# Two views of the rows, 64 bytes apart, and weights that begin 64 bytes later

## The reference

```
y = modulate(rmsnorm(h), sh, sc);  h = h + 0.5 * gt * swiglu(y, w_gu, w_down)     # D_FF = 2816
proj = modulate(rmsnorm(h), ...) @ w_in        # q, k, v, gu, gv: attention and gated mixing
h = h + gt2 * (merged @ w_out);                # then a second swiglu, then rmsnorm
```

## Time and profile before

| | us |
|---|---|
| median of 3 runs | 2518.12 (2514.95 to 2522.17) |
| the profiled execution, its own time | 2518.71 |
| its span, from first to last instruction | 2516.9 |
| TensorE matmuls busy | 2442.9 (97%) |
| VectorE busy | 1515.5 (60%) |
| ScalarE busy | 893.3 (35%) |
| GpSimd busy | 380.7 (15%) |

### The profile page before, as it was taken

The page is one execution under the profiler, slowest core; times in us unless marked ns, Lnnn a source line. Parts: engine busy times, 40 slices in busy tenths (PEclk is TensorE's granted clock), DMA queues, the critical chain, the costliest instruction groups (busy, mean ns, idle before and its releaser), DMA issues.

```text
span 2516.9 us, 39335 instructions
## 1 busy us (share of the span) xinstructions
PE 2442.9 (97%) x14736; PEld 2165.5 (86%) x14736; DVE 1515.5 (60%) x2434; ACT 893.3 (35%) x1103; POOL 380.7 (15%) x353
## 2 busy tenths in 40 slices
PE   6999989999999998999999999999999999999999
PEld 5998879999888888867778888888888889999999
DVE  7676767967877765355477776642222364555444
ACT  4443554444222223332232222232222242254443
POOL 2110531211111102332211111001110001000110
PEclk7999989999999999999999999999999999999999
DMA  7877745854655554211135545422222342234545
GB/s 279 277 260 268 260 140 199 272 196 167 209 192 200 175 167 153 80 63 51 67 119 198 197 170 191 161 101 89 94 84 97 104 143 84 68 118 151 184 168 166
DMA packets 79878, 400.19 MB, mean 159 GB/s; under 512 B 8816, under 2 KB 12912, under 8 KB 54704
## 3 DMA queue, kind: packets, MB, share of 16 engines
q1 hardware_dynamic: 77216, 393.39, 45.3%
q0 software_dynamic: 1056, 3.67, 0.4%
q10 hardware_dynamic: 1520, 1.95, 0.2%
HBM read 396.88 MB, written 2.10 MB: 159 GB/s over the span
## 4 chain that ended last, share of the span: by engine, by line
PE 85%; DVE 7%; ACT 3%; DMA 3%; issue 2%; POOL 0%; ACTq 0%; SPq 0%; DVEq 0%; POOLq 0%
PE pg L1159 24%; PE pg L1161 24%; PE pg L1160 24%; DMA raw<-w_d 2%; PE pg L1335 2%; PE pg L1336 2%; PE pg L1337 2%; DVE wlo L2049 1%; PE px L1977 1%; DMA raw<-w_t 1%; ACT whi L662 1%; DVE ada L2089 1%; PE px L1738 1%; PE pg L1777 1%; PE px L1963 1%
## 5 line engine op out<-in xcount | busy, mean ns | idle before, releaser
L1159 PE MATMUL pg<-Yh,whi 128*128 128x256 f32 (+1 forms) x2856 | 958.6, 336 | 27.5 <-DVE Yl L2209 7.6
L1160 PE MATMUL pg<-Yl,whi 128*128 128x256 f32 (+1 forms) x2856 | 948.5, 332 | 0.0
L1161 PE MATMUL pg<-Yh,wlo 128*128 128x256 f32 (+1 forms) x2856 | 948.3, 332 | 0.0
L2054 DVE TENSOR_TENSOR wlo<-raw,whi 128x2048 fp32r<-128x2048 f32 (+1 forms) x202 | 415.0, 2055 | 517.7 <-ACT whi L667 517.0
L1159 PEld LDWEIGHTS pg<-Yh,whi 128*128 128x128 f32 x2856 | 548.0, 192 | 90.4 <-issue 20.9
L1161 PEld LDWEIGHTS pg<-Yh,wlo 128*128 128x128 f32 x2856 | 548.1, 192 | 50.1
L1160 PEld LDWEIGHTS pg<-Yl,whi 128*128 128x128 f32 x2856 | 548.4, 192 | 49.0
L667 ACT ACTIVATE whi<-raw 128x2048 fp32r<-128x2048 f32 (+1 forms) x202 | 348.4, 1725 | 563.8 <-PE pg L1161 521.8
L1159 PE MATMUL pg<-Hh,whi 128*128 128x256 f32 (+1 forms) x1122 | 368.9, 329 | 4.7 <-DVE wlo L2054 3.2
L1160 PE MATMUL pg<-Hl,whi 128*128 128x256 f32 (+1 forms) x1122 | 366.4, 327 | 0.0
L1161 PE MATMUL pg<-Hh,wlo 128*128 128x256 f32 (+1 forms) x1122 | 366.4, 327 | 0.0
(11 more groups left out here) (352 smaller groups left out, 2354.8 us busy)
## 6 DMA issues: line engine op xcount, KB each, us to landing
raw<-w_t SPq DMA_DIRECT2D x194, 1024.0 KB, 5.0
ada<-w_ada SPq DMA_DIRECT2D x200, 512.0 KB, 3.6
raw<-w_d SPq DMA_DIRECT2D x96, 704.0 KB, 4.1
ADA<-w_ada SPq DMA_DIRECT2D x16, 512.0 KB, 14.6
NB<-na_bias POOLq DMA_DIRECT2D x8, 256.0 KB, 2.9
X<-x_t ACTq DMA_DIRECT2D x2, 512.0 KB, 16.7
spectrum<-HF POOLq DMA_DIRECT2D x1, 1024.0 KB, 9.2
X<-ctx_t SPq DMA_DIRECT2D x1, 1024.0 KB, 7.4
```

The source lines that it names most:

```text
L1159: pe.matmul(out, w_hi, y_hi, start=first, stop=False)
L1160: pe.matmul(out, w_hi, y_lo, start=False, stop=False)
L1161: return pe.matmul(out, w_lo, y_hi, start=False, stop=last)
L2054: dve.tensor_tensor(wlo[:, n % 2, 0:size], raw[:, n % 2, 0:size], whi[:, n % 2, 0:size].bitcast(F32), ALU.subtract)\
```

## The change

No instruction is added, removed or moved. The tensors' places change:

- A second view of the rows, YhB and YlB, begins 64 bytes after Yh and Yl, and a second view of the hidden rows, HhB and HlB, 64 bytes after Hh and Hl. Each pair shares its memory; 128 bytes of room follow each tensor.
- `row_view(name)` gives the B views for the norms and phases in SHORT_ROWS, that is where the phase has 256 columns, and for l1_in, whose products have 512 columns only for k; otherwise the views as before. `inner_of(name)` does the same for the hidden rows by the phase's column count. All writes and reads of the rows go through them.
- raw, whi and wlo begin 64 bytes past a multiple of 128, and another 64 bytes follow wlo, so that ada and all behind it keep their place modulo 128.
- The tensors of layer 1's mixer (K3, VN3 and those behind, with OH and OL laid over them) begin 64 bytes later in the region.
- HF, DF0 and HP, which use idle halves of the rows' memory early on, move with the B views.

```diff
@@ -183,6 +183,8 @@
 
     return 18 * list(LEAD).index(name) + {"added": 1, "inverse": 2, "scaled": 2 * c + 2 if c else 3, "lo": min(2 * c + 5, 18)}[step]
 
+SHORT_ROWS = ("b1_0", "b1_gu1", "b1_1", "b1_in", "merge", "b1_out", "b1_2", "b1_gu2", "l1_1", "l1_in", "l1_2", "l1_gu2")
+
 READS = {"b1_gu1": "b1_0", "b1_in": "b1_1", "b1_out": "merge", "b1_gu2": "b1_2", "l0_gu1": "l0_0", "l0_in": "l0_1",
          "l0_gu2": "l0_2", "l1_gu1": "l1_0", "l1_in": "l1_1", "l1_gu2": "l1_2"}
 
@@ -204,10 +206,17 @@
     X = sb("X", [P, KD, 512])
     y_at = at[0]
     Yh = sb("Yh", [P, 4096], F32R)
+    YhB = nc.alloc_sbuf_tensor_at("YhB", [P, 4096], F32R, offset=y_at + 64)
+    at[0] += 128
+    yl_at = at[0]
     Yl = sb("Yl", [P, 4096], F32R)
+    YlB = nc.alloc_sbuf_tensor_at("YlB", [P, 4096], F32R, offset=yl_at + 64)
+    at[0] += 128
+    at[0] += 64
     raw = sb("raw", [P, 2, BLK])
     whi = sb("whi", [P, 2, BLK], F32R)
     wlo = sb("wlo", [P, 2, BLK], F32R)
+    at[0] += 64
     ada = sb("ada", [P, 2, KD * P])
     V = sb("V", [P, NVEC])
     MOD = sb("MOD", [P, 216, 2])
@@ -225,15 +234,21 @@
     def over(): at[0] = region
 
     Hh = sb("Hh", [P, KF, 512], F32R)
+    HhB = nc.alloc_sbuf_tensor_at("HhB", [P, KF, 512], F32R, offset=region + 64)
+    at[0] += 128
+    hl_at = at[0]
     Hl = sb("Hl", [P, KF, 512], F32R)
+    HlB = nc.alloc_sbuf_tensor_at("HlB", [P, KF, 512], F32R, offset=hl_at + 64)
+    at[0] += 64
+    assert at[0] <= end
 
     over()
     EMB = sb("EMB", [64, 256]); FW1 = sb("FW1", [64, 64]); FW23 = sb("FW23", [64, 2, 64]); FW4 = sb("FW4", [64, 1024])
     FA = sb("FA", [64, 256]); FK = sb("FK", [64, 256]); FS = sb("FS", [64, 3, 256])
     WIN = sb("WIN", [P, 2, 512]); HN = sb("HN", [P, 2, 1024]); CS = sb("CS", [P, 1024])
-    HF = nc.alloc_sbuf_tensor_at("HF", [P, 8, 512], F32, offset=y_at)[:, :, 256:512]
-    DF0 = nc.alloc_sbuf_tensor_at("DF0", [P, 8, 512], F32, offset=y_at + 16384)[:, 2:6, 256:512]
-    taps = nc.alloc_sbuf_tensor_at("HP", [P, 22, 512], F32, offset=region)
+    HF = nc.alloc_sbuf_tensor_at("HF", [P, 8, 512], F32, offset=y_at + 64)[:, :, 256:512]
+    DF0 = nc.alloc_sbuf_tensor_at("DF0", [P, 8, 512], F32, offset=yl_at + 64)[:, 2:6, 256:512]
+    taps = nc.alloc_sbuf_tensor_at("HP", [P, 22, 512], F32, offset=region + 64)
 
     def HP(part):
         return taps[:, 14 + 4 * part:18 + 4 * part, 256:512]
@@ -292,7 +308,15 @@
 
     def rhs_r(t):
         return t[:, :].rearrange("p (c n) -> p c n", n=256)
-    Yh8, Yl8, Yh16, Yl16 = rhs_t(Yh), rhs_t(Yl), rhs_r(Yh), rhs_r(Yl)
+    Yh8, Yl8, YhB8, YlB8 = rhs_t(Yh), rhs_t(Yl), rhs_t(YhB), rhs_t(YlB)
+
+    def row_view(name):
+
+        return (YhB8, YlB8) if name in SHORT_ROWS else (Yh8, Yl8)
+
+    def inner_of(name):
+
+        return (HhB, HlB) if INFO[name][2] == 256 else (Hh, Hl)
 
     def vcol(name, i=0, rows=P):
         return V[0:rows, VEC[name] + i:VEC[name] + i + 1]
...
@@ -523,8 +548,8 @@
                 with pool.Fori(0, KF // 2) as j:
                     for u in range(2):
                         pool.wait_ge(sem["h_hi"], j * 2 + (k + u + 1))
-                        pool.tensor_tensor(Hl[:, bass.ds(j * 2 + u, 1), 0:tokens], TMP[:, u:u + 1, 0:tokens],
-                                           Hh[:, bass.ds(j * 2 + u, 1), 0:tokens].bitcast(F32), ALU.subtract)\
+                        pool.tensor_tensor(inner_lo[:, bass.ds(j * 2 + u, 1), 0:tokens], TMP[:, u:u + 1, 0:tokens],
+                                           inner_hi[:, bass.ds(j * 2 + u, 1), 0:tokens].bitcast(F32), ALU.subtract)\
                             .then_inc(sem["h_lo"], 1)
 
             ctx_square, ctx_sum = TMP[:, 1, 256:512], TMP[:, 0, 256:512]
...
@@ -1286,6 +1311,7 @@
                 evac, ebase = EVAC[name]
                 blocks, ebase = blocks - first, ebase + first
                 if mode == "d":
+                    inner_hi, inner_lo = inner_of(name)
                     h_before = KF * [f.replace("gu", "down") for f in FFNS].index(name) + CREDIT
                     def four(j, pairs=(0, 1)):
                         for v in pairs:
@@ -1298,7 +1324,7 @@
                                     if v == 0 and (half, kt) in ((0, 0), (1, 0), (1, 9), (1, 10)):
                                         pe.wait_ge(sem["h_lo"], h_before + (11 if half == 0 else 20 if kt == 0 else 12 + kt))
                                     last = three(pg[v][:, 0, 0:tokens], whi[:, half, w], wlo[:, half, w],
-                                                 Hh[:, 11 * half + kt, 0:tokens], Hl[:, 11 * half + kt, 0:tokens],
+                                                 inner_hi[:, 11 * half + kt, 0:tokens], inner_lo[:, 11 * half + kt, 0:tokens],
                                                  half == 0 and kt == 0, half == 1 and kt == 10)
                                 last.then_inc(sem["pe_block"], 1)
                     if name == "b1_down2":
@@ -1328,7 +1354,7 @@
                             for half in range(2):
                                 w = slice(256 * kt + P * half, 256 * kt + P * half + P)
                                 last = three(pg[u][:, half, 0:tokens], whi[:, u, w], wlo[:, u, w],
-                                             Yh8[:, kt, 0:tokens], Yl8[:, kt, 0:tokens], kt == 0, kt == 7)
+                                             row_view(name)[0][:, kt, 0:tokens], row_view(name)[1][:, kt, 0:tokens], kt == 0, kt == 7)
                         last.then_inc(sem["pe_block"], 1)
 
             def three_moving(out, w_hi, w_lo, y_hi, y_lo, first, last):
...
@@ -1931,14 +1957,14 @@
                         out = pg[u][:, tt // 2, 256 * (tt % 2):256 * (tt % 2) + 256]
                         for kt in range(8):
                             w, y = slice(256 * kt, 256 * kt + 256), slice(P * tt, P * tt + P)
-                            last = three_moving(out, whi[:, u, w], wlo[:, u, w], Yh8[:, kt, y], Yl8[:, kt, y], kt == 0, kt == 7)
+                            last = three_moving(out, whi[:, u, w], wlo[:, u, w], row_view("l1_in")[0][:, kt, y], row_view("l1_in")[1][:, kt, y], kt == 0, kt == 7)
                 else:
                     tokens = 512 if kind == "k" else 256
                     for kt in range(8):
                         for half in range(2):
                             w = slice(256 * kt + P * half, 256 * kt + P * half + P)
                             last = three(pg[u][:, half, 0:tokens], whi[:, u, w], wlo[:, u, w],
-                                         Yh8[:, kt, 0:tokens], Yl8[:, kt, 0:tokens], kt == 0, kt == 7)
+                                         row_view("l1_in")[0][:, kt, 0:tokens], row_view("l1_in")[1][:, kt, 0:tokens], kt == 0, kt == 7)
                 last.then_inc(sem["pe_block"], 1)
 
             def turn_qk(k):
@@ -2204,12 +2230,12 @@
                 def lo(c):
                     dve.wait_ge(sem["y_hi"], yb + c + 1)
                     for s, cols in streams(tokens):
-                        hi_part = Yh8[:, c + post, cols].bitcast(F32)
+                        hi_part = row_view(name)[0][:, c + post, cols].bitcast(F32)
                         if shift:
-                            ins = dve.scalar_tensor_tensor(Yl8[:, c + post, cols], TMP[:, c % 2, cols], shift(c, s), hi_part,
+                            ins = dve.scalar_tensor_tensor(row_view(name)[1][:, c + post, cols], TMP[:, c % 2, cols], shift(c, s), hi_part,
                                                            ALU.add, ALU.subtract)
                         else:
-                            ins = dve.tensor_tensor(Yl8[:, c + post, cols], TMP[:, c % 2, cols], hi_part, ALU.subtract)
+                            ins = dve.tensor_tensor(row_view(name)[1][:, c + post, cols], TMP[:, c % 2, cols], hi_part, ALU.subtract)
                     ins.then_inc(sem["y_lo"], 1)
                 for c in range(k):
                     if c >= 2:
...
```

More of the change, by code:

```diff
@@ L709, in norm @@
                     for s, cols in streams(tokens):
-                        ins = act.activation(Yh8[:, c + post, cols], TMP[:, c % 2, cols], ACT.Identity, bias=shift(c, s)) \
-                            if shift else act.activation(Yh8[:, c + post, cols], TMP[:, c % 2, cols], ACT.Copy)
+                        ins = act.activation(row_view(name)[0][:, c + post, cols], TMP[:, c % 2, cols], ACT.Identity, bias=shift(c, s)) \
+                            if shift else act.activation(row_view(name)[0][:, c + post, cols], TMP[:, c % 2, cols], ACT.Copy)
                     ins.then_inc(sem["y_hi"], 1)
@@ L727, in lead_norm @@
                     act.wait_ge(sem["lead_dve"], lead_dve(name, "scaled", c))
-                    act.activation(Yh8[:, c, 0:256], TMP[:, c % 2, 0:256], ACT.Identity, bias=shift(c, 0)).then_inc(sem["lead_act"], 1)
+                    act.activation(row_view(name)[0][:, c, 0:256], TMP[:, c % 2, 0:256], ACT.Identity, bias=shift(c, 0)).then_inc(sem["lead_act"], 1)
                     if c == 3:
@@ L747, in rest_hi @@
```

(13 more changed lines are left out.)

12 lines of the change are left out of this document (6 added, 6 removed).

## The result

The changed kernel takes 2532.73 us (median of 6 runs, 2529.49 to 2536.74) beside 2517.27 us before (6 runs, 2514.95 to 2522.17). The ratio is 1.006, with an interval from 1.0047 to 1.0074: slower by 0.6%, where 1.1% faster was forecast. The profiled execution has a span of 2534.9 us against 2516.9.

What follows compares the result with a forecast made beforehand. TensorE's matmul pitch in the 512-column stages was taken as the bound. 2518.7 - 33.4 (512-column matmuls) + 6.6 (256-column ones in long phases) = 2491.9 us, 2491.3 against the median, stated as 2491.5; range 2460 to 2530.

Steps and rivals of the forecast that it cites:

- What bounds the kernel: 512-column stages: TensorE has no gap, so a change of time between matmuls reaches the kernel's end one for one.
- The premise: fp32r matmuls: 13.3 ns over the columns is not fixed, but two reads (moving operand, next weights) disturbing each other, alterable by address.
- rival (a): All fp32r matmuls: the extra 13.3 ns belongs to fp32r itself, so nothing changes, 2518 us; chance 0.25 with small shifts.
- the sentence quoted from the Trainium skill: TensorE: loading the next weights steals no SBUF read bandwidth from the running matmul; by that the address is free, sum 0.
- lock on that period: 5010 512-column matmuls: pitch locks on 128 bytes of moving stream; half a period's shift saves 6.7 ns each, 33.4 us.
- Rival (c): 512-column matmuls: 0 apart is the good lock, 64 apart the bad; pitch 232.5 ns, 2554 us; chance 0.18.
- 0 apart again: Short 256-column phases, some 7,100 matmuls: operands keep distance 0 modulo 128, so 120.0 ns as now, 0 us.
- The absolute address: Short 256-column phases: operands stand at another absolute address; priced at nothing without a row, one ns would be 7 us.
- The 256-column matmuls in the long phases: 993 matmuls now 64 apart: pitch goes up to 126.7 ns, 6.6 us lost; the other end was 113.3 ns.
- The other terms at nothing: VectorE's and ScalarE's passes cost the same at any of these addresses, and raw's blocks still land in 5.0 us: 0.

Runs made afterwards that it cites:

- e8: TensorE-only probe with fifteen widths, alike and weights 64 past, plus plain fp32; 504 columns alike take 226.7 ns, plain fp32 429.2 and 215.8 ns a record.
- e1: Probe with only TensorE working, 55 stretches of 144 fp32r matmuls at varied start addresses; all alike 226.7 ns at 512 columns, 120.0 at 256.
- e7: TensorE-only probe with the stationary operand 128, 64 and 32 columns wide; at 512 columns alike 226.7, 229.9 and 231.7 ns.
- e6: TensorE-only probe over all combinations of starts in 64-byte steps, each twice; at 512 columns 226.7 ns all alike, otherwise 228.7 to 235.4.
- e2: Kernel before the change with only raw, whi and wlo 64 bytes later, high and low rows alike; 2532.39 us beside 2514.80, ratio 1.0059.
- e5: Changed kernel with 256 instead of 128 bytes of room between high and low parts, so they start alike; 2546.06 us beside 2516.86, ratio 1.0127.
- e3: Kernel before the change with only 128 bytes of room put behind Yh, Yl and Hh, weights left in place; 2529.16 us beside 2514.80, ratio 1.0053.
- e4: Changed kernel with the two views exchanged and high and low parts alike; 2503.58 us beside 2516.86 for the kernel before, ratio 0.9943.

## Why the prediction was wrong

**What bounds the kernel** held. The long stages passed the pitch on: the 3624 matmuls of the normed rows by 4.4 ns and the 1386 of the hidden rows by 3.7 ns are 21 us, less about 2 us for the 993 shorter ones. The eight stages grew by 23.2; of the 4 us left the clock's drop in l0_in is about 3.

**The premise** held in part. Plain fp32 has its 2.5 ns at all four sets of starts tried (e8), the fp32r extra isn't fixed, and it moves with the distances of the starts, also with TensorE alone (e1). That refutes rival (a), and with it the use I made of the sentence quoted from the Trainium skill, "TensorE: Matmul & The Clock Gate", Part 2: the same instructions take 226.7 to 235.4 ns with nothing but their start addresses changed. Whether the reading of the weights is what is in the way no run shows; e7 rules out only that the extra shrinks with the load's width. The cause inside TensorE stays open.

**The step that failed is the "lock on that period"**, priced at 5010 x 6.7 ns saved. From two pitches, each the columns plus 32, I made a period of 128 bytes, and from it a shift downwards, since there was room below. The 32 columns, 13.3 ns, are no constant: alike, the extra is 11 to 22 ns over fifteen widths (e8). The distances repeat at 256 bytes and not at 128, and all alike is the lowest pitch at 512 columns that any of e1's or e6's starts reached: there was no way down, and every departure in steps of 64 bytes costs 2 to 9 ns. The change's price was +4.4 ns for the normed rows and +3.7 for the hidden ones, not -6.7. Rival (c) had this mechanism and from the earlier trace rows a price of 232.5, within 1.5 ns of the measured 231.1; I gave it 0.18 because after a start such pitches drift back to 226.7. That row is of a place where the starts are alike, so the drift spoke of the good place before, and not against a bad one after: in e2 and e5 the steady pitch itself is 233.3.

**"0 apart again" was read modulo 128.** So I called the 128 bytes of room between Yh and Yl, and between Hh and Hl, nothing, and the short phases unchanged. By e3 that room alone costs 0.53%. In the change it is one of two shifts that soften each other (e5 has 1.27%, the change 0.6%), and it is why the short products of the normed rows went to 118: with high and low alike they stay at 120.0 (e5). The short products of the hidden rows stayed at 120.0 even so, because there the low rows are alike with the weights and the high ones lie 128 before them; e1 has 120.0 for those starts too. The absolute address, the doubt I had named for these phases, is worth nothing at the places tried. Of the roughly 11 us that the other 5,600 short products could give, the short stages and l1_in show 7.8.

**The 256-column matmuls in the long phases** were forecast at 126.7 ns and went to 118, below the 120.0 of before and not above it. I had taken the 7 ns above a bare load for a wall on that side. With high and low alike, 64 bytes is in fact the best distance at 256 columns: 113.3 ns (e1), which is the pitch I had named as the end of the range.

**The other terms at nothing** were right: VectorE's 2297 ns, the landings of 5.0 us, ScalarE and GpSimd.

## What to carry to other kernels

Where TensorE never pauses, read the pitch from the starts, and vary the operands' starts modulo 256 bytes in a small kernel with TensorE alone before moving a tensor: here that kernel gave 231.1, 230.4, 117.8 and 120.0 ns for the four sets of starts at which the changed kernel shows 231.1, 230.4, 118 and 120. Repeat each set, since some give two answers, and compute the starts of every operand group modulo 256: room put in one place moves all that follows. For fp32r products in this order with 512 columns keep high rows, low rows and both weights alike modulo 256; with 256 columns let both weights begin 64 bytes past the rows (113.3 ns in the small kernel, 113.5 to 117.8 by stage in e2 and e4, against 120.0); and give the room between a high and a low part in whole multiples of 256. A pitch that looks like a lock tells neither its period nor on which side of it there is room: two points on one address are no slope.
